# An encoder layer's feed-forward outputs: copied by ScalarE and summed by adding DMAs in HBM, instead of added by VectorE in SBUF

## The reference

```python
h = _rms(x, norm1_g)
q, k, v, c = jnp.split(h @ w_in, ...)
attn = _window_attention(q, k, v, attn_sink)
u = silu(layernorm(dwconv31(a * sigmoid(gate))))
x = x + jnp.concatenate([attn, u], axis=-1) @ w_out
h2 = _rms(x, norm2_g)
g = jax.nn.silu(_dwconv(h2 @ ffn_w_gate, ffn_dw_w, ffn_dw_b))
x = x + (g * (h2 @ ffn_w_up)) @ ffn_w_down
```

## Time and profile before

| | us |
|---|---|
| runs of the kernel before (3) | 2582.58 median, 2579.39 to 2584.51 |
| profiled execution: span from the first to the last instruction | 2578.6 |
| profiled execution: its own time as the runs give it | not on its page |
| TensorE busy | 2556.6 (99%) |
| VectorE busy | 1861.8 (72%) |
| ScalarE busy | 1250.3 (48%) |
| GpSimd busy | 184.7 (7%) |
| HBM | 328.01 MB read, 88.77 MB written |

### The profile page before, as it was taken

One profiled execution on the slowest core, in us unless ns is written; L12 is line 12 of the kernel. 1 busy time (PEld: TensorE's weight loads), 2 busy tenths in 40 slices (PEclk: granted clock), 3 DMA queues, 4 the chain that ended last, 5 costly groups with the idle time before them and its releaser, 6 DMA issues. The chain is left out here.

```text
span 2578.6 us, 35519 instructions
## 1 busy us (share of the span) xinstructions
PE 2556.6 (99%) x12927; PEld 2287.9 (89%) x12927; DVE 1861.8 (72%) x3100; ACT 1250.3 (48%) x2166; POOL 184.7 (7%) x316
## 2 busy tenths in 40 slices
PE   8999999999999999999999999999999999999999
PEld 6877777788878887888888899999999999999999
DVE  4776658887888697968884687657667875765765
ACT  6345544468337844683563444335335443533532
POOL 0110021101011111110101100000000100000000
PEclk9999999999999999999999999999999999999999
DMA  9967789734554465447439542222223522221212
GB/s 350 348 229 237 261 290 345 276 112 164 205 206 137 146 246 212 162 159 263 155 122 357 178 148 68 66 60 68 66 61 116 171 66 62 66 66 61 67 58 70
DMA packets 139757, 419.11 MB, mean 163 GB/s; under 512 B 24160, under 2 KB 38880, under 8 KB 122944
## 3 DMA queue, kind: packets, MB, share of 16 engines
q1 hardware_dynamic: 113632, 317.93, 36.5%
q0 software_dynamic: 25952, 98.92, 10.0%
HBM read 328.01 MB, written 88.77 MB: 162 GB/s over the span
## 5 line engine op out<-in xcount | busy, mean ns | idle before, releaser
L1477 ACT ACTIVATE part_hi<-part_raw 128x512 fp32r<-128x512 f32 x396 | 247.6, 627 | 387.7 <-DMA part_raw<-w_pass_t 158.4
L2224 PE MATMUL bank<-hw_hi,weights 128*128 128x462 f32 (+3 forms) x1408 | 420.8, 373 | 0.0
L1751 DVE SCALAR_TENSOR_TENSOR cc<-win,par,cc 128x512 f32<-128x512 f32 x600 | 408.4, 745 | 0.0
L2384 PE MATMUL bank<-mid,part_hi 128*128 128x414 f32 x1408 | 376.9, 348 | 2.5 <-DVE mid L1986 2.0
L1930 DVE TENSOR_TENSOR part_lo<-part_raw,part_hi 128x512 fp32r<-128x512 f32 x396 | 271.0, 689 | 136.1 <-ACT part_hi L1477 130.6
L2175 PE MATMUL bank<-h_hi,weights 128*128 128x512 f32 x1104 | 354.6, 394 | 0.0
L2224 PEld LDWEIGHTS bank<-hw_hi,weights 128*128 128x128 f32 x1408 | 264.9, 188 | 37.0 <-issue 12.2
L2384 PEld LDWEIGHTS bank<-mid,part_hi 128*128 128x128 f32 x1408 | 263.3, 188 | 4.3 <-DVE mid L1986 3.4
L2224 PE MATMUL bank<-hw_lo,weights 128*128 128x464 f32 (+3 forms) x704 | 259.3, 368 | 0.0
L2175 PEld LDWEIGHTS bank<-h_hi,weights 128*128 128x128 f32 x1104 | 207.3, 188 | 51.2 <-issue 5.9
L2370 PE MATMUL bank<-T_hi,part_hi 128*128 128x414 f32 (+1 forms) x704 | 246.2, 350 | 0.5 <-DVE e L1954 0.5
(11 more groups left out here) (221 smaller groups left out, 4283.0 us busy)
## 6 DMA issues: line engine op xcount, KB each, us to landing
weights<-weight_scratch SPq DMA_DIRECT2D x88, 1024.0 KB, 6.0
wraw<-w_ffn_t SPq DMA_DIRECT2D x88, 512.0 KB, 3.5
part_raw<-w_ffn_t SPq DMA_DIRECT2D x176, 256.0 KB, 2.7
weight_scratch<-weights POOLq DMA_DIRECT2D x22, 1024.0 KB, 7.7
wraw<-w_down_t SPq DMA_DIRECT2D x44, 512.0 KB, 3.5
part_raw<-w_pass_t SPq DMA_DIRECT2D x88, 256.0 KB, 2.6
cat_hi<-cat_scratch SPq DMA_DIRECT2D x10, 1024.0 KB, 6.8
cat_lo<-cat_scratch SPq DMA_DIRECT2D x10, 1024.0 KB, 8.9
```

What stands on the lines that cost most here:

```text
L1477: nc.scalar.activation(p_hi[k % HI_RING][:], p_raw[part_of(k)][:], ACT.Copy).then_inc(s_whi, 1)
L1751: nc.vector.scalar_tensor_tensor(acc, win[i][:, tap:tap + TB], w_tap, acc, ALU.mult, ALU.add).then_inc(s_cv, 1)
L2224: mm = nc.tensor.matmul(out, l[:, k, :], r[:, k, cols], start=(k == 0 and j == 0), stop=(k == KT - 1 and j == 2))
L2384: mm = nc.tensor.matmul(bank[BANK_Y[n % 4]][:, 0:TP], l[:, (deep * o + t) % KH, :], mid2[:, t, part, i, :], start=(t == 0 and z == 0), sto ...
```

## The change

- `pair_y_add` on VectorE goes, with the two big tiles `yb2`. In its place ScalarE copies each output from its bank to one of four small tiles `y_out[n % 4]` (`pair_y_copy`), at the head of the same list entry.
- GpSimd's queue issues one DMA for each of the 192 outputs, which adds the tile to the output array `y` in HBM (`add_pair_y`, `accum_op=ALU.add`). The 32 final stores go.
- The copy of output n waits until the adding DMA of output n-4 has landed (`s_yadd[n % 4]`). TensorE's wait on `s_y` is now a wait for ScalarE's copy.
- x2 has to be in `y` before the adds: chunks 2 to 4 are stored there instead of in `x2_d`, and of chunk 1 the last 119 columns are stored a second time, there. One padding column of `y` is set to zero. The four loads of `pair_y` go.
- The residual loads of the plain windows share semaphores in twos.

```diff
 PAD_SPANS = ((0, 1), (1 + PROMPT, 1), (2 + TOKENS, PAD_COLS - TOKENS - 2))
-ZERO_STORES = 4 + 2 * len(PAD_SPANS)
+Y_PADS = OUT_COLS - TOKENS - 1
+ZERO_STORES = 4 + 2 * len(PAD_SPANS) + 1
...
+Y_PAIR = 2 * KT * len(PASSES) * PAIRS
+PAIR_START = sum(WIDTH)
...
 for _k in DOWNS:
-    DVE_AT[_k + 1].insert(0, ("y_add", _k))
+    ACT_AT[_k + 1].insert(0, ("y_copy", _k))
...
-    for _w in range(2):
-        SP_AT[at(GROUPS * _q, 2)].append(("y", _q, _w))
...
-        yb2 = [run(o, (f"pair_y{i}", [P, KT, TP], F32))[0] for i, o in enumerate(y_at)]
+        y_out = [run(o + V_BYTES * j, (f"pair_y{2 * i + j}", [P, TP], F32))[0] for i, o in enumerate(y_at) for j in range(2)]
...
-        s_yl = [sem(f"y_residual_loaded{i}") for i in range(KT)]
+        s_yl = [sem(f"y_residual_loaded{i}") for i in range(KT // 2)]
         s_y = sem("y_ready")
         s_yst = [sem(f"y_stored{i}") for i in range(KT)]
-        s_ylast = sem("last_y_stored")
+        s_x2y = sem("x2_stored_in_y")
+        s_yadd = [sem(f"pair_y_added{i}") for i in range(4)]
...
-                sp.dma_start(yb[:, o, 0:WIDTH[w]], x2_d[o, :, 1 + window_start(w):1 + window_start(w + 1)]).then_inc(s_yl[o], 16)
+                sp.dma_start(yb[:, o, 0:WIDTH[w]], x2_d[o, :, 1 + window_start(w):1 + window_start(w + 1)]).then_inc(s_yl[o // 2], 16)
...
-            def load_pair_y(q, i):
-                if q > 0:
-                    sp.wait_ge(s_yst[i], 16 * (PLAIN + KT * q))
-                else:
-                    for o in range(KT):
-                        sp.wait_ge(s_yst[o], 16 * PLAIN)
-                w = PLAIN + 2 * q + i
-                sp.wait_ge(s_x2st, x2_stores(needs_chunk(w)))
-                sp.dma_start(yb2[i][:], x2_d.rearrange("k p n -> p k n")[:, :, 1 + window_start(w):1 + window_start(w) + TP]) \
-                  .then_inc(s_yl[i], 16)
...
-            def store_last_y(i, o):
-                w = PLAIN + 2 * (PAIRS - 1) + i
-                sp.wait_ge(s_y, Y_PLAIN + pair_output(PAIRS - 1, i, o) + 1)
-                sp.dma_start(y[o, :, window_start(w):window_start(w) + TP], yb2[i][:, o, :]).then_inc(s_ylast, 16)
...
-            pads = [(d.rearrange("k p n -> p k n"), a, w) for d in (x2_d, h2_d) for a, w in PAD_SPANS]
+            pads = [(d.rearrange("k p n -> p k n"), a, w) for d in (x2_d, h2_d) for a, w in PAD_SPANS] + [(y.rearrange("k p n -> p k n"), OUT_COLS - Y_PADS, Y_PADS)]
...
             def store_x2(c, o):
                 pool.wait_ge(s_x2, KT * c + o + 1)
-                pool.dma_start(x2_d[o, :, padded(c):padded(c) + TB], x2[c][:, o, :]).then_inc(s_x2st, 16)
+                if c < 2:
+                    pool.dma_start(x2_d[o, :, padded(c):padded(c) + TB], x2[c][:, o, :]).then_inc(s_x2st, 16)
+                if c == 1:
+                    pool.dma_start(y[o, :, PAIR_START:padded(1) - 1 + TB], x2[1][:, o, PAIR_START - padded(1) + 1:TB]) \
+                        .then_inc(s_x2y, 16)
+                if c >= 2:
+                    pool.dma_start(y[o, :, padded(c) - 1:padded(c) - 1 + TB], x2[c][:, o, :]).then_inc(s_x2st, 16)
 
...
-            def store_pair_y(q, i, o):
-                n = pair_output(q, i, o)
+            def add_pair_y(q, n, o, i):
                 w = PLAIN + 2 * q + i
                 pool.wait_ge(s_y, Y_PLAIN + n + 1)
-                pool.dma_start(y[o, :, window_start(w):window_start(w) + TP], yb2[i][:, o, :]).then_inc(s_yst[i], 16)
-
-            for q in range(PAIRS - 1):
-                for o in range(KT):
-                    for i in (1, 0):
-                        store_pair_y(q, i, o)
+                pool.dma_start(y[o, :, window_start(w):window_start(w) + TP], y_out[n % 4][:],
+                               accum_op=ALU.add).then_inc(s_yadd[n % 4], 16)
+
+            pool.wait_ge(s_zst, 16 * ZERO_STORES)
+            pool.wait_ge(s_x2y, 16 * KT)
+            pool.wait_ge(s_x2st, x2_stores(CHUNKS - 1))
+            for k in DOWNS:
+                for n, o, i in y_outputs(k):
+                    add_pair_y(PROD[k][1], n, o, i)
             for o in range(KT):
                 pool.wait_ge(s_yst[o], 16 * PLAIN)
-            for i in range(2):
-                pool.wait_ge(s_yst[i], 16 * (PLAIN + KT * (PAIRS - 1)))
+            for i in range(4):
+                pool.wait_ge(s_yadd[i], 16 * Y_PAIR // 4)
...
+            def pair_y_copy(k):
+                for z, (n, o, i) in enumerate(y_outputs(k)):
+                    if z == len(y_outputs(k)) - 1:
+                        act.wait_ge(s_used, SLOTS + k + 1)
+                    else:
+                        act.wait_ge(s_dn, DN_PLAIN + n + 1 - DOWN_AT[k])
+                    if n >= 4:
+                        act.wait_ge(s_yadd[n % 4], 16 * (n // 4))
+                    elif n == 0:
+                        for o_ in range(KT):
+                            act.wait_ge(s_yst[o_], 16 * PLAIN)
+                    nc.scalar.activation(y_out[n % 4][:], bank[BANK_Y[n % 4]][:, 0:TP], ACT.Copy).then_inc(s_y, 1)
...
-                    dve.wait_ge(s_yl[o], 16 * (w + 1))
+                    dve.wait_ge(s_yl[o // 2], 32 * (w + 1))
...
-            def pair_y_add(k):
-                q, F = PROD[k][1:3]
-                for z, (n, o, i) in enumerate(y_outputs(k)):
-                    if z == len(y_outputs(k)) - 1:
-                        dve.wait_ge(s_used, SLOTS + k + 1)
-                    else:
-                        dve.wait_ge(s_dn, DN_PLAIN + n + 1 - DOWN_AT[k])
-                    if F == 0:
-                        dve.wait_ge(s_yl[i], 16 * (PLAIN + q + 1))
-                    else:
-                        dve.wait_ge(s_y, Y_PLAIN + n - 2 * KT + 1)
-                    nc.vector.tensor_tensor(yb2[i][:, o, :], bank[BANK_Y[n % 4]][:, 0:TP], yb2[i][:, o, :], ALU.add) \
-                      .then_inc(s_y, 1)
```

More of the change, by code:

```diff
@@ L596, in encoder_layer @@
         B_PITCH, P_PITCH = pitch(TQ), pitch(TP)
-        B_BYTES, E_BYTES, V_BYTES, W_BYTES, Y_BYTES = 4 * KH * B_PITCH, up256(4 * TQ), up256(4 * TP), 4 * KH * P, up256(4 * KT * TP)
+        B_BYTES, E_BYTES, V_BYTES, W_BYTES, Y_BYTES = 4 * KH * B_PITCH, up256(4 * TQ), up256(4 * TP), 4 * KH * P, 2 * up256(4 * TP)
         M_BYTES = 4 * 4 * 2 * 2 * P_PITCH
@@ L828, in y_outputs @@
                     for o in range(per * j, per * (j + 1)) for i in range(2)]
-        def pair_output(q, i, o):
-            return 2 * KT * (len(PASSES) * (q + 1) - 1) + 2 * o + 1 - i
         def gu_index(w, h, i):
@@ L1067, in _ @@
                         load_pair_window(t[1], t[2])
-                    elif t[0] == "y":
-                        load_pair_y(t[1], t[2])
-            for o in range(KT):
-                for i in (1, 0):
-                    store_last_y(i, o)
-            sp.wait_ge(s_ylast, 16 * 2 * KT)
         @block.gpsimd
@@ L1636, in _ @@
                         part_high(t[1])
+                    elif t[0] == "y_copy":
+                        pair_y_copy(t[1])
                     elif t[0] == "window_high":
@@ L2121, in _ @@
                         part_sum(t[1], t[2])
-                    elif t[0] == "y_add":
-                        pair_y_add(t[1])
                     elif t[0] == "window_sum":
```

## The result

The changed kernel takes 2595.28 us (median of 4 runs, 2591.06 to 2598.72) against 2582.43 (4 runs, 2579.39 to 2584.51): ratio 1.0049, 95% interval 1.0035 to 1.0063. Five more executions later (the ninth experiment) gave 2591.94 against 2581.49, ratio 1.0045 [1.0031, 1.0059]. So it is slower by 0.45 to 0.5%, 10 to 13 us. That lies inside the predicted range, but not in the case that the prediction held likeliest ("within 0.2%"): it is its first rival, the stalled short passes.

What follows compares the result with a forecast made beforehand. TensorE was taken as the bound, so VectorE's relief buys almost nothing. Terms: 0.3 (short-pass wait) - 0.46 (recovered wait) + 0 + 2.1 (end) = +2 us on 2582.58, giving 2585; range 2580 to 2603.

Steps and rivals of the forecast that it cites:

- within 0.2%: Whole kernel: time changes by less than 0.2%, 5.2 us, either way; chance 0.56.
- first rival: Short passes: add landings stall TensorE, the end grows too; 5.5 us at landing 5.2, about +20 at 8; chance 0.23.
- The ten deep passes: Outputs come every 2.24 us, four in 8.96; landings up to 8.1 us cost nothing, term 0.
- The moves of the first part: Stores of x2 and chunk 1's last 119 columns into y, changed residual loads: 0 us.
- L: Time from issue to landing of an adding DMA: taken as 4.2 us, bounds 2.6 and 6.3.
- 2C - 9.7: First short pass: TensorE's wait at output 12, C being one tile's round (copy, 0.30, L), 5.0 us: 0.3 us.
- 2C - 11.4: Second short pass: TensorE's wait at output 12, C being one tile's round, 5.0 us: below zero, so 0.
- The threshold of 5.2 us: Landing time of the adds from which the first rival decides, with 5.5 us lost in all.
- the median of all adds: Sign, issue to landing of small-tile DMAs: 4.2 us forecast; over 5.2 the first rival holds, over 9 the second rival.
- The second rival: All passes: adding DMAs can't keep up, over 2.24 us of all engines each or L over 9.4; about 2690; chance 0.15.
- Issue of an adding DMA: GpSimd's queue: each issue keeps 0.54 us, not stretched by VectorE's work, so the queue keeps up.
- The end: After TensorE's last matmul: copy, issue and a 3.8 us landing replace SP's store, +2.1 us on the span.

Runs made afterwards that it cites:

- the ninth experiment: The changed kernel run again unaltered, for more executions and a second profile: 2591.94 us, ratio 1.0045 to the kernel before.
- the doubled run: Against the changed kernel, each adding DMA followed by a second from the same tile into unread scratch columns, 384 in all: 2619.1 us, one execution.
- e11_tail4: The changed kernel with four tiles, its last two outputs loaded and stored by SP and added by VectorE as before: 2589.07 us, ratio 1.0031.

## Why the prediction was right in its range and wrong in its likeliest case

**What held.** VectorE's relief is worth nothing: no kernel here is measurably faster than the one before. The copies are hidden at 518 ns. The ten deep passes cost 0 (375.00 of 375 us, and the run with plain stores in the short passes alone). The moves of the first part, taken as 0, cost between nothing and 0.13%. The landing, 4.2 us by an estimate between 2.6 and 6.3, was 4.0 in the median over all adds.

**The step that failed: one L for every place.** The prediction worked out the short passes with the landing of 4.2 us, which is that of a deep pass. In the short passes it is 5.4 and 6.2: an add takes about 1.25 us of all engines where they stand back to back (six tiles and the doubled run), and 1.12 us is all there is, with the weights' loads beside it (12 to 19% of the engines). With each pass's own L the formula gives 2C - 9.7 = 2.7 and 2C - 11.4 = 2.6 us, and TensorE's waits are 2.1 and 2.6. The passes cost more than these waits, 2.8 and 5.2 us by the marks above: 1.6 of the 5.2 are the clock (below), and short gaps make up the rest. The formula also has TensorE stop first at output 12; in the trace it stops first at output 8, 9.8 us into the pass:

```profile
1539.16 0.62 PE L2368 MATMUL bank<-mid,part_hi 128*128 128x414 f32 x2 [0.62 <-ACT pair_y L1513]
```

So its frame held, and its price was low.

The threshold of 5.2 us was crossed in just the passes for which it was set, while the median of all adds, named as the sign to look for, stayed at 4.0 and would have spoken for the forecast. A latency read in one stretch must be asked again for the stretch whose rate is twice as high. The second rival had asked that question (does an add take more than its share of the engines?) but set it against 2.24 us, the deep pass, and priced three passages at 1.7 us for that; against 1.12 even that price says that the short passes fall behind. The rule that it cites from the Trainium skill ("DMA: Bandwidth & Descriptors", Issuing engines are not separate DMA queues) is borne out: in 2079 to 2101 SP's 256 KB loads landed in 5.5 us, and in 3.2 in the same pass of the kernel with plain stores.

**In part luck.** The range held because it took in rival 1 up to a landing of 8 us. For a landing of 5.8, the mean of both passes, that rival's sum is 3.5 + 1.8 + 3.7 - 0.5 = 8.5 us, 2591, close to the measured 2592 to 2595. But it has the end grow with L, and there the landing stayed at 3.8; what it overcharges there stands in for the clock, the gaps and the close of the program, which it doesn't have.

**Issue of an adding DMA: 0.54 us predicted, 0.85 measured** (0.54 again once the adding is taken out). It isn't contention with VectorE: the last add was issued in 0.85 us with VectorE idle, and the plain stores in 0.54 with VectorE at work. So the rule of the Trainium skill ("SBUF — State Buffer", Who interferes with whom) was rightly given no weight here; the same section says that VectorE's two-input sums were not seen to stall DMAs. The landing is counted from the start of the issue, so the 0.3 us lie within L and add nothing to the round or the end. They count only where issues stand in line: the first four adds of the first short pass were issued one behind the other in 3.50 us.

**The end: +2.1 us predicted, +3.3 measured.** The copy, the 0.3 us to the issue and the landing (3.8 us) were right; what was left out is that the span ends 1.7 us after this landing of GpSimd's queue and 0.5 after that of SP's, the whole difference. Removed as a whole in the kernel with the old end, it is worth 2.9 us with four tiles.

**Not in the prediction: the clock.** Behind the 2.56 us wait TensorE worked for 3.4 us at the lower level, 1.6 us more. It raised the price of one short pass in one of three profiles with four tiles.

**Sum by the runs.** From the median 2582 (before): short passes 7 to 10 (changed kernel against eight tiles, 2591.94 or 2595.28 less 2584.9), end 3, first part 0 to 3. Measured as a whole it is 10 to 13, so the first part lies at the low end of its range. The prediction's terms for the same were -0.2, +2.1 and 0.

## What to carry to other kernels

Before a sum moves from an engine into adding DMAs, set the time that one add takes of all DMA engines, back to back, against the shortest spacing at which it is asked for, not against the mean: here 1.25 against 1.12 us cost 0.3 to 0.4% in two passes of twelve, and with two or four more small tiles TensorE no longer waited. Where the engine that is relieved isn't the bound, the best such a change can do is come out level. Keep the last outputs off the long way: two outputs done by VectorE and SP were worth 3 us.

## What the runs showed of the hardware

- An adding DMA of 207 KB from SBUF into HBM takes 1.76 us of all 16 engines' time where one is asked for every 2.24 us and 1.24 to 1.27 us where they stand back to back; a plain store of the same takes 0.54 (at one every 2.24). At half the bytes it is 1.0, with rows of twice the length 1.50 for the same bytes.
- Its issue on GpSimd's queue takes 0.85 us in the median, at half and at twice the bytes too, that of the store 0.54. It grows where the queue is full: 1.00 us in the median in the first short pass with eight tiles, 1.18 for the second adds of the doubled run.
- It lands in 3.9 us in a deep pass. In the first short pass it is 5.4 with four in flight, 7.2 with six, 9.0 with eight; in the second 6.2, 6.7 and 6.5.
- The granted clock fell to half, for 3.4 us, behind one wait of 2.56 us, and behind waits of 1.9 to 3.2 in seven profiles; it did not behind waits of 2.1 and 2.7 in two others, nor behind one of 1.5 (e11_tail4). In the doubled run it fell behind waits of 1.32 and 1.23 us that came soon after others (2.63; 0.82, 0.82 and 1.02). No length of a wait by itself told whether it would.
- The span ended 1.4 to 1.9 us after the last landing where that was of GpSimd's queue and awaited there, and 0.5 after it where it was of SP's.
